# Index scores of the last tile moved to ScalarE and GpSimd, sample scores in column groups, bias from 32 DRAM copies

## The reference

```python
# dsa_attend, for a block of queries
scores = relu(einsum('bqhd,bkd->bqhk', qi, idx_keys))   # 8 heads of width 64
scores = einsum('bqhk,bqh->bqk', scores, wi) * IDX_SCALE
topk   = 128 of the prompt keys (prompt), 256 of 1025 past keys (sample)
logits = q.k * ATTN_SCALE + t5_bias(table, q_pos - idx)  # bias depends on distance and head
out    = softmax(logits) @ v
```

## Time and profile before

| | before |
|---|---|
| median of 3 runs | 1205.15 us (1205.14 to 1206.71) |
| profiled execution, own time | 1203.8 us |
| its span | 1202.1 us |
| granted TensorE clock, mean | 0.993 |
| PE busy | 1157.5 us, 96% |
| DVE busy | 890.4 us, 74% |
| ACT busy | 558.9 us, 46% |
| POOL busy | 92.3 us, 8% |

### The profile page before, as it was taken

One profiled execution on the slowest core, in us unless ns is written; L12 is line 12 of the kernel. 1 busy time (PEld: TensorE's weight loads), 2 busy tenths in 40 slices (PEclk: granted clock), 3 DMA queues, 4 the chain that ended last, 5 costly groups with the idle time before them and its releaser, 6 DMA issues.

```text
span 1202.1 us, 24762 instructions
## 1 busy us (share of the span) xinstructions
PE 1157.5 (96%) x9294; PEld 1064.4 (89%) x9294; DVE 890.4 (74%) x1759; ACT 558.9 (46%) x1012; POOL 92.3 (8%) x141
## 2 busy tenths in 40 slices
PE   8999988999999999999999999899999999999995
PEld 4959844589999999999999988699999999999995
DVE  2279999857899488597677766768895795795676
ACT  2342158844654353443334566744642443543334
POOL 4425400200000000000510000000000000000000
PEclk9999989999999999999999999999999999999998
DMA  7599480043223324233533221141223223233222
GB/s 214 181 283 291 150 255 23 21 156 108 71 71 107 88 87 140 71 100 112 157 92 104 83 63 42 32 147 63 71 75 120 87 106 95 82 106 105 90 86 71
DMA packets 64048, 132.38 MB, mean 110 GB/s; under 512 B 7835, under 2 KB 36667, under 8 KB 63819
## 3 DMA queue, kind: packets, MB, share of 16 engines
q1 hardware_dynamic: 47899, 115.16, 29.9%
q10 hardware_dynamic: 12688, 9.31, 2.6%
q0 software_dynamic: 3360, 6.56, 1.7%
HBM read 126.46 MB, written 9.79 MB: 113 GB/s over the span
## 4 chain that ended last, share of the span: by engine, by line
PE 78%; DVE 14%; ACT 2%; issue 2%; SPq 2%; DMA 1%; ACTq 0%; DVEq 0%
PE PS L704 34%; PE PS L901 20%; PE PS L736 12%; PE PS L1219 3%; PE PS L1031 2%; PE PS L987 2%; PE PS L972 2%; SPq L479 2%; PE PS L1001 1%; DVE SC L2477 1%; DVE MX L2475 1%; DVE PB L2303 1%; DVE MSK L2486 1%; DMA KVX<-cacheV 1%; DVE YA L2162 1%
## 5 line engine op out<-in xcount | busy, mean ns | idle before, releaser
L704 PE MATMUL PS<-XH,WHI 128*128 128x260 f32 x1088 | 221.5, 285 | 0.7 <-DVE XL L2346 0.7
L704 PE MATMUL PS<-XH,WLO 128*128 128x260 f32 x1088 | 219.1, 283 | 0.0
L704 PE MATMUL PS<-XL,WHI 128*128 128x260 f32 x1088 | 218.8, 283 | 0.0
L704 PEld LDWEIGHTS PS<-XH,WHI 128*128 128x128 f32 x1088 | 167.5, 188 | 5.9 <-issue 4.8
L704 PEld LDWEIGHTS PS<-XH,WLO 128*128 128x128 f32 x1088 | 167.6, 188 | 0.0
L704 PEld LDWEIGHTS PS<-XL,WHI 128*128 128x128 f32 x1088 | 167.3, 188 | 0.0
L1281 ACT ACTIVATE WHI<-WRAW 128x1024 fp32r<-128x1024 f32 x72 | 76.2, 1059 | 178.5 <-PE PS L704 138.5
L1823 DVE TENSOR_TENSOR WLO<-WRAW,WHI 128x1024 fp32r<-128x1024 f32 x64 | 79.2, 1238 | 98.4 <-ACT WHI L1281 98.3
L901 PE MATMUL PS<-HH,RNH 128*128 128x260 f32 x384 | 109.0, 284 | 2.5 <-DVE RNL L1963 2.4
L901 PE MATMUL PS<-HL,RNH 128*128 128x260 f32 x384 | 108.4, 282 | 0.0
L901 PE MATMUL PS<-HH,RNL 128*128 128x260 f32 x384 | 108.3, 282 | 0.0
(11 more groups left out here) (349 smaller groups left out, 2790.0 us busy)
## 6 DMA issues: line engine op xcount, KB each, us to landing
WRAW<-wall SPq DMA_DIRECT2D x168, 512.0 KB, 3.6
bias_skewed<-bias_seq SPq DMA_DIRECT2D x4, 1280.0 KB, 18.3
BT<-bias_skewed ACTq DMA_DIRECT2D x3, 1024.0 KB, 9.0
X<-xT SPq DMA_DIRECT2D x4, 520.0 KB, 6.6
X<-xT SPq DMA_DIRECT2D x1, 2080.0 KB, 11.3
yT<-X SPq DMA_DIRECT2D x8, 260.0 KB
KVB<-cacheK SPq DMA_DIRECT2D x16, 128.0 KB, 3.1
KVX<-cacheK SPq DMA_DIRECT2D x16, 128.0 KB, 3.3
```

Source lines behind the costliest of these rows:

```text
L704: mm = pe.matmul(PS[:, 2 * slot + g, 0:TG], tile, x[:, k, TG * g:TG * g + TG], start=(k == 0 and w is w_hi and x is hi), stop=(k == KT - 1 ...
```

## The change

1. **Index products in fours.** The 24 items go between the first six slices of unit 5 in groups of four.
2. **The last tile leaves DVE.** For tile 3, ACT puts the eight ReLUs into eight buffers (`SC` and `RS3`, seven slots that lie over `UQ` 7 to 13). After `DS` it multiplies each by its head's weight (`weigh_last_tile`), and POOL adds seven of them into `SC` (`add_heads`), three before the low part of unit 8 and four after it. ACT's copies to `UQ` from unit 7 on wait for `is_pool`.
3. **Sample scores in column groups.** Four blocks of 32 columns write four groups of 32 rows of PSUM, each product by itself, and `SR`, `WD` and `WB` have 128 rows. The constants are 64 columns longer.
4. **DVE's order.** `sample_queries` and the low part of unit 6 come after tile 2; scaling and causal mask of a tile (`finish_scores`) come just ahead of its first round; 5 rounds in place of 10 stand before the digits, 7 and 8 in place of 5 and 5 after `mask_done`.
5. **POOL's order.** The `QB` memset stands behind the adds, and the pages behind the low parts of units 9 to 12, two each.
6. **Bias.** 32 copies, each displaced by four elements, written by one DMA; each read is four DMAs, one for every fourth partition.

```diff
-SKEW = 768
+SKEW, QUART = 768, 32
+        def bias_columns(eng, to, c0, c1, done):
+            for i in range(P // QUART):
+                eng.dma_start(to[i::P // QUART], bskew[:, :, 127 - i + c0:127 - i + c1]
+                              ).then_inc(done, 16)
...
-            pool.wait_ge(ds_mm, 3)
-            nc.gpsimd.memset(QB[:], 0.0).then_inc(z_qb, 1)
-            for pg in range(4):
-                load_page(pool, 3, pg)
+            def add_heads(h0, h1):
+                for h in range(h0, h1):
+                    pool.wait_ge(is_scaled, h + 1)
+                    if h > 1:
+                        pool.wait_ge(is_pool, h - 1)
+                    nc.gpsimd.tensor_tensor(SC[:, 2, :], SC[:, 2, :], RS3[:, h - 1, 0:SEQ], ALU.add
+                                            ).then_inc(is_pool, 1)
+            add_heads(1, 4)
             for u in range(POOL_LO[0], A_OUT):
                 low_part(u, u % 2)
-                if u < POOL_LO[0] + 4:
-                    load_page(pool, 3, 4 + u - POOL_LO[0])
+                if u == POOL_LO[0]:
+                    add_heads(4, IDXH)
+                    nc.gpsimd.memset(QB[:], 0.0).then_inc(z_qb, 1)
+                else:
+                    for pg in range(2 * (u - POOL_LO[0] - 1), 2 * (u - POOL_LO[0])):
+                        if pg < NPG:
+                            load_page(pool, 3, pg)
...
                     for c in range(4):
-                        mm = pe.matmul(PSF[0:HD, 2048 + c0:2048 + c1],
-                                       QB[:, HD * c:HD * c + HD], IK[:, c, c0:c1],
-                                       start=(c == 0), stop=(c == 3))
+                        r = slice(32 * c, 32 * c + 32)
+                        mm = pe.matmul(PSF[r, 2048 + c0:2048 + c1], QB[:, r], IK[:, c, c0:c1],
+                                       start=True, stop=True)
...
-                    between = {k: (lambda k=k: index_scores(3 * k, 3 * k + 3))
-                               for k in range(KT)}
+                    between = {k: (lambda k=k: index_scores(4 * k, 4 * k + 4))
+                               for k in range(len(items) // 4)}
...
+            def weigh_last_tile():
+                act.wait_ge(is_relu, 3 * IDXH)
+                for h in range(IDXH):
+                    x = RS3[:, h - 1, 0:SEQ] if h else SC[:, 2, :]
+                    nc.scalar.activation(x, x, ACT.Copy, scale=NAT[:, 3, HD + h:HD + h + 1]
+                                         ).then_inc(is_scaled, 1)
...
                     act.dma_start(ORD[:], io["ord"]).then_inc(ord_in, 16)
+                    weigh_last_tile()
...
-            for n, (t, h) in enumerate(items):
-                if n == 8:
-                    low_part(6, 0)
-                if n == 16:
-                    sample_queries()
+            for n, (t, h) in enumerate(items[:2 * IDXH]):
...
+            sample_queries()
+            low_part(6, 0)
...
-            prompt_rounds(10)
+            prompt_rounds(5)
             low_part(7, 1)
             dve.wait_ge(ds_ev, 1)
...
-            prompt_rounds(5)
+            prompt_rounds(7)
             dve.wait_ge(z_qb, 2)
...
-            prompt_rounds(5)
+            prompt_rounds(8)
```

More of the change, by code:

```diff
@@ L218, in constants @@
     for b in range(DB):
-        c[b, C_WD + 8 * b:C_WD + 8 * b + 8] = 1.0
+        at = C_WD + 32 * (b // 2) + 8 * (b % 2)
+        c[b, at:at + IDXH] = 1.0
         c[NH * b:NH * b + NH, C_SAM + b] = 1.0
@@ L580, in _ @@
             sp.wait_ge(toe_out, 16)
[L581 to L585, removed]
+            sp.dma_start(bass.AP(tensor=bskew.tensor, offset=0,
+                                 ap=[[NH * SKEW + P // QUART, QUART], [SKEW, NH], [1, 640]]),
+                         bass.AP(tensor=bseq.tensor, offset=0,
+                                 ap=[[0, QUART], [640, NH], [1, 640]])).then_inc(toe_skew, 16)
             early(POOL_LO[0] // 2, 1)
-            sp.wait_ge(toe_skew, 16 * 4)
+            sp.wait_ge(toe_skew, 16)
             sp.wait_ge(is_relu, 3 * IDXH)
             sp.wait_ge(ds_mm, 3)
-            sp.dma_start(BT0[:], bskew[:, :, 127 + 384:127 + 512]).then_inc(toe_in[0], 16)
+            bias_columns(sp, BT0[:], 384, 512, toe_in[0])
             late = (12,) + V_HALF + V_LATE
@@ L1657, in _ @@
                         act.wait_ge(is_mm, n + 1)
-                        if n >= 2:
+                        if 2 <= n < 2 * IDXH:
                             act.wait_ge(is_acc, n - 1)
-                        nc.scalar.activation(RS[:, n % 2, 0:(t + 1) * P],
-                                             PS[:, 4 + n % 4, 0:(t + 1) * P], ACT.Relu
+                        if n == 2 * IDXH:
+                            act.wait_ge(toe_out, 16)
+                        to = (RS[:, n % 2, 0:(t + 1) * P] if t < 3 else
+                              RS3[:, h - 1, 0:SEQ] if h else SC[:, 2, :])
+                        nc.scalar.activation(to, PS[:, 4 + n % 4, 0:(t + 1) * P], ACT.Relu
                                              ).then_inc(is_relu, 1)
@@ L1677, in _ @@
                     high_part(u + 2, u % 2)
+                if u >= 7:
+                    act.wait_ge(is_pool, min(u - 6, IDXH - 1))
                 if u < 6:
@@ L1693, in _ @@
                         WB[:].rearrange("p (b h) -> p b h", b=DB),
-                        PS[0:HD, 6, 0:DB].rearrange("p (b o) -> p b o", o=1).broadcast_to(
-                            [HD, DB, NH]), ACT.Copy).then_inc(wb_ev, 1)
+                        PS[:, 6, 0:DB].rearrange("p (b o) -> p b o", o=1).broadcast_to(
+                            [P, DB, NH]), ACT.Copy).then_inc(wb_ev, 1)
                 if u == 3:
@@ L2456, in _, with finish_scores @@
                 dve.wait_ge(is_acc, n + 1)
-            for t in range(1, QT):
+            sample_queries()
+            low_part(6, 0)
+            def finish_scores(t):
+                if t == 3:
+                    dve.wait_ge(is_pool, IDXH - 1)
                 V.tensor_scalar(SC[:, t - 1, 0:t * P], SC[:, t - 1, 0:t * P], float(ISCALE), None,
@@ L2474, in prompt_halves @@
                     if half == 0:
+                        if i == 0:
+                            finish_scores(t)
                         after(V.max(MX8[:], sc))
```

40 lines of the change are left out of this document (20 added, 20 removed).

## The result

The changed kernel takes 1213.81 us (median of 5 runs, 1212.36 to 1214.61); the kernel before, in 5 runs beside it, 1205.15 us. The ratio is 1.0074, 95% interval 1.0062 to 1.0085: 0.7% slower, 8.7 us on the medians. Forecast were 5.5 us (1210.6 us). The measured median lies inside the stated range of 1202.0 to 1216.0 and 0.8 us above what the prediction calls the forecast's own range, 1208 to 1213. The profiled execution takes 1212.36 us with a span of 1210.7 us; before, its span was 1202.1 us, so the spans differ by 8.6 us.

What follows compares the result with a forecast made beforehand. PE was taken to bound the kernel from 63 to 143 us and DVE to set the pace from 139 us; 0.4 + 6.25 + 0.6 - 0.2 - 1.5 = +5.5 us on 1205.15 gave 1210.6 us, range 1202.0 to 1216.0.

Steps and rivals of the forecast that it cites:

- So `SR` comes 7.85 us after unit 5.: Sample scores: ACT's 14 page-number reads still stand ahead of the ReLU `SR`, which starts at 88.25, not 82.
- rival 1: ACT's reads do not hold the ReLU `SR`: end at 1203.4 us, chance 0.08, or 1200.5 us, chance 0.12.
- PE's gap of 5.0 us: Ahead of the sample sums PE stops at 83.85 and waits for the first ReLU until 88.85.
- the price of 2.1 us: Cost of the granted clock falling after PE's gap ahead of the sample sums: 2.1 us, bounds 0 and 2.1.
- DVE's hole of 10.5 us: After low part 7, at 83.6, DVE idles 10.5 us for `DS`.
- Rounds moved out of the hole and tile 3's scaling: DVE behind `mask_done`: 15 rounds instead of 10 add 6.25 us, tile 3's scaling 0.6 us.
- The add of 1.43 us: Each 512-wide POOL add takes 1.43 us, bounds 0.71 and 2.4; low part 9 then ends at 112.9.
- Rivals 2 and 3: POOL's adds cheap, 0.71 to 1.1 us, end 1206 to 1208.5, chance 0.22; or slow, 2.4 us, end 1218, chance 0.10.
- DVE's digits, now beside 256-wide rounds only, keep ahead of PE, so the old waits go.: In units 7 to 13 PE's two waits of 0.56 us for DVE's digits vanish, 1.2 us.
- `mask_done` 0.4 us later, at 139.45.: After unit 13, whose slot is at 137.7 against 137.28, `mask_done` comes 0.4 us later.
- The prompt attention is one chain ... and carries it on whole.: From step 2 on, the chain between DVE, ACT and PE passes on the whole delay of 5.5 us.
- Bias 0: ACT's bias issues, grown from one to four of 0.53 us each, cost 0; without DVE's longer chain covering them, up to 3 us.

Runs made afterwards that it cites:

- e1: Changed kernel with ACT's 14 page-number reads moved from ahead of `SR` to ahead of its waits for units 9 and 10; 1206.94 us, 1.0007 of the kernel before.
- e4: Changed kernel with four more products of 512, to an unused bank, in PE's gap ahead of the sample sums; 1212.75 us, 1.0065 of the kernel before.
- e3: Changed kernel with POOL's seven adds cut from 512 columns to 32, for timing alone; 1210.92 us, 1.0043 of the kernel before.
- g3: Changed kernel with tile 3's weighted sums made by DVE in its wait for `DS`, without ACT's weighing or POOL's adds; 1209.69 us, 1.0042 of the kernel before.
- e2: Changed kernel with DVE's rounds back in the earlier places, 10, 5 and 5 for 5, 7 and 8; 1209.58 us, 1.0041 of the kernel before.
- g1: Changed kernel with page-number reads moved to units 9 and 10, rounds 8, 6, 6, late bias reads issued by SP; 1202.30 us, 0.9980 of the kernel before.
- f4: Kernel before with only ACT's 14 page-number reads moved to units 9 and 10; 1206.14 us, 0.9996 of the kernel before.
- g2: Kernel before with the bias part and its eight late reads issued by SP instead of ACT; 1204.87 us, 0.9993 of the kernel before.
- f1: Kernel before with the bias part alone, 32 copies and four reads in place of one; 1207.26 us, 1.0008 of the kernel before.
- f2: Kernel before with only the products in fours and the sample scores in column groups; 1206.45 us, 1.0005 of the kernel before.
- f5: Changed kernel with the bias part undone, four writes of 1280 KB and one read each; 1214.10 us, 1.0074 of the kernel before.

## Why the prediction was right, and where it was off

The direction and the mechanism held; the sum of 5.5 us is 3.0 too small against the marker's 8.57, more than a third of what was measured. The largest part of that, 1.75 us, is a term that was put at nothing, and a fall of the clock at step 2 goes with it. Point by point, by the prediction's own steps:

- *"So `SR` comes 7.85 us after unit 5."* Right: 89.03 against 81.1, 7.9 us. e1 shows that the reads do it, which rules out rival 1 (that they don't hold the ReLU) by an experiment.
- *PE's gap of 5.0 us, the price of 2.1 us, DVE's hole of 10.5 us.* Right: 4.95, 1.9 (3.98 less 2.10; e4 shows that it is the gap) and 10.11 us. The upper bound of 2.1 us was too low: in e3 and g3, with the same gap, the sums take 4.00 us and the matmuls behind them are slow as well, so that from the end of the sums to unit 7 it is 5.0 and 4.8 us and not 4.24, up to 0.8 us more.
- *Rounds moved out of the hole and tile 3's scaling: from `mask_done` to step 2 5.15 us more.* Right: 36.33 us before, 41.19 after, 4.86 more. e2 takes the rounds back and gets 5.3 us at the marker.
- *The add of 1.43 us.* It takes 1.28 to 1.38 us. Rivals 2 and 3 had it cheaper or slower; POOL is through with low part 9 at 113.95 (predicted 112.9).
- *"DVE's digits, now beside 256-wide rounds only, keep ahead of PE, so the old waits go."* **This step failed.** The rounds are indeed short, but the small two-input operations of the digits are held while POOL adds, and PE waits 0.64 and 1.25 us for them. POOL's wait shrinks to 0.97 us (predicted 3.1), because PE is late by then. In all PE waits 2.86 us, where the forecast had 3.1; so this failure alone moved the sum little. It matters for the cure: e3 and g3 give 3 us back by removing the adds.
- *"`mask_done` 0.4 us later, at 139.45."* It is 140.99. Of the 1.5 us too much, unit 7 brings 0.5 (97.91, predicted 97.4; unit 5's first products start 0.37 later in this execution than before, 63.92 against 63.55, and from there to the scores 2.0 us are won where 2.4 were forecast), tile 2's scaling 0.58 (the rows at 138.27 and 138.47): the scalings were moved into the rounds, and with five rounds fewer ahead of the digits that of tile 2 falls into the last digit step, on the path. With 8 or 10 rounds there (g1, e2) the distance from the last slot to the mask is 0.98 us and not 1.57. The prediction counted tile 3's scaling only. Some 0.7 us more lie spread over units 7 to 13, less 0.2 us by which PE's waits are shorter than forecast; they go with PE's waits, each of which costs some 0.15 to 0.35 us more than its bracket says. In g3, which has no such wait, PE needs 36.90 us from unit 7's slot to unit 13's; the kernel before needs 38.39 with two waits of 1.18 us in all, the changed kernel 40.75 with three of 2.86.
- *"The prompt attention is one chain ... and carries it on whole."* **A term put at nothing, and the largest error:** from step 2 to the marker it takes 45.94 us and not 44.19, 1.75 us more. DVE no longer waits 1.52 us for PE ahead of step 2; instead PE waits 3.42 us for DVE (the prediction says itself that PE's logits lie before DVE's being free, so that PE stands there), the granted clock falls, the turn takes 1.97 us and not 1.09, and behind it DVE waits 1.33 us for the next logits. The prediction priced such a fall for the gap ahead of the sums and, as a possibility, for unit 9 (where it did not come), but not here. The other traces bear this out. In f4 and g2, where the clock holds at 1.00 and ACT has no more bias reads to issue than before, this stretch takes 44.19 and 44.18 us. In all eight traces in which the clock falls at step 2 it takes 45.3 to 46.5. In e1, e2 and f1 the clock holds too, but ACT's eight issues delay the eviction, and it takes 45.29, 46.62 and 46.28; in e1 PE waits 2.01 us ahead of step 2, and of its 1.1 us the late eviction has 0.8. f2 is the nearest to a test, since it has the bias of the kernel before and no adds on POOL: PE waits 2.57 us, the clock is at 0.50 from 178 to 181, and the stretch takes 45.32. No run was made for this alone.
- *Bias 0, "without that cover up to 3 us".* Both right: f5 shows 0 with the cover, f1 and e2 2.1 us without it (and e1, with part of the cover, 0.8: the eviction starts at 176.55, PE's turn ended at 175.75).

Added up: 1.96 (`mask_done`) + 4.86 + 1.75 = 8.57 us.

## What to carry to other kernels

A faster product gains nothing if the engine that takes its result has something else in its queue: read what stands there ahead of the consumer before you count the gain. Work that an engine does in a wait is free (6 us of it in g3), and taking it away buys nothing; what decides is on which side of the wait the rest of its work stands, and here five rounds on the wrong side cost 5 us. Offloading from VectorE to GpSimd cost VectorE's two-input operations here whatever was left of GpSimd's current instruction, so long GpSimd instructions don't belong beside a chain of small dependent ones. And where a change makes TensorE wait at a new place, count a possible fall of its clock at each such place, not only at the first.

## What the runs showed of the hardware

- A VectorE operation on one element a partition with two SBUF inputs took 1.16 and 1.21 us instead of 0.16 beside a GpSimd add, and ended 0.02 us behind it each time; beside GpSimd's memset it took 0.16.
- It goes the other way too: in f4 two pieces of a low part on GpSimd (128x256, two inputs) took 1.71 and 1.70 us beside VectorE's two-input operations over 1025 columns, and the next two, with those over, 0.73 and 0.72; one of the two VectorE operations took 1.65 us and not 1.29.
- Four matmuls of 512 columns on alternating halves of 64 rows took 1.99 us, three took 1.98. The sample scores took 1.97 us as products of 32 columns in four column groups, and 7.49 us as products of 64 columns.
- Whether the clock falls at one place differs between these executions. In layer 1's attention PE stands some 1.5 us in both of these. Timelines of PE, the kernel before and e1:

```profile
756.35 1.09 PE L987 MATMUL PS<-CST,PBB 128*128 128x128 f32 x8 [1.54 <-DVE PBB L2339]
...
757.78 2.05 PE L1233 MATMUL PS<-BT,QBB 128*128 128x128 f32 x16
```

```profile
756.58 1.80 PE L1007 MATMUL PS<-CST,PBB 128*128 128x128 f32 x8 [1.44 <-DVE PBB L2375]
...
759.03 3.78 PE L1253 MATMUL PS<-BT,QBB 128*128 128x128 f32 x16
```

After a pause of 1.54 us the sixteen records take 2.05 us; after one of 1.44 us the granted clock is at 0.50 and they take 3.78. The length of the pause does not decide it: in the changed kernel it is 1.44 us and the clock holds, in f1 1.54 us and the clock falls. In all twelve profiled executions of experiments these sixteen records take 3.36 to 3.78 us; in those of the kernel before and the changed kernel 2.05. From the marker to their end it is 540.3 us in these two and 541.7 to 543.3 in the twelve. So totals of single executions differ by up to 3 us at this place, 537 us behind the marker. That it is chance is not shown by these traces, since each kernel has one; the kernel before, unedited, had mean granted clocks from 0.991 to 0.995 in the 21 executions beside g1 to g3, so its clock does vary from one execution to the next.
